# Second block's attention: heads in pairs, the rotary scores of an even and an odd head one right behind the other

## The reference, cut to what matters

```python
k = jnp.concatenate([k_nope, jnp.broadcast_to(k_rope[:, :, None, :], (b, l, MLA_HEADS, QK_ROPE_DIM))], axis=-1)
...
def one(qblk):                                  # blocks of 128 queries
    sc = jnp.einsum('bqhd,bkhd->bhqk', qblk, k, preferred_element_type=jnp.float32) * scale
    p = jax.nn.softmax(sc, axis=-1).astype(v.dtype)
    return jnp.einsum('bhqk,bkhd->bqhd', p, v)
```

## Time and profile before

| | |
|---|---|
| Time, 3 runs | 2943.76 us median, 2937.95 to 2945.43 |
| The profiled execution | 2945.6 us, of which its span 2943.5 us |
| Busy share of the span | PE 97%, PEld 84%, DVE 69%, ACT 39%, POOL 3% |
| Mean granted TensorE clock | 0.986 of full speed |
| Stage of the change | 998.11 to 1056.20 us of the span |

### The profile page before, as it was taken

How to read it: one execution, slowest core, us unless ns; L and a number is a source line. 1 busy time by engine, 2 the same in 40 slices (tenths; PEclk the granted TensorE clock), 3 DMA queues, 4 the chain that set the end, 5 groups by cost and what they waited for, 6 DMA issues and landing times.

```text
span 2943.5 us, 51456 instructions
## 1 busy us (share of the span) xinstructions
PE 2849.0 (97%) x19824; PEld 2462.9 (84%) x19824; DVE 2043.5 (69%) x3896; ACT 1139.3 (39%) x1795; POOL 86.2 (3%) x96
## 2 busy tenths in 40 slices
PE   8998999998999999999999999988999999999997
PEld 7885998885996669998999999865999999999986
DVE  4755884764874559997666666774999766666667
ACT  2423552432553432234444444431323444444443
POOL 0012000022000000000000000000000000000000
PEclk9999999999999999999999999999999999999999
DMA  5204883303883224424555555653442455555564
GB/s 197 101 18 175 326 314 129 115 32 115 314 326 145 86 90 162 152 88 175 183 181 181 183 184 185 237 191 143 148 166 76 166 184 183 185 185 185 183 227 154
DMA packets 79283, 498.30 MB, mean 169 GB/s; under 512 B 9264, under 2 KB 13744, under 8 KB 22320
## 3 DMA queue, kind: packets, MB, share of 16 engines
q1 hardware_dynamic: 70080, 477.73, 44.6%
q10 hardware_dynamic: 9072, 18.72, 1.8%
HBM read 485.92 MB, written 10.49 MB: 169 GB/s over the span
## 4 chain that ended last, share of the span: by engine, by line
PE 95%; DVE 3%; issue 1%; POOL 1%; ACT 1%; DMA 0%; DVEq 0%; SPq 0%; ACTq 0%; POOLq 0%
PE bank L841 24%; PE bank L853 24%; PE bank L887 7%; PE bank L2047 5%; PE bank L521 4%; PE bank L1860 4%; PE bank L2085 4%; PE bank L2094 4%; PE bank L671 3%; PE bank L738 2%; PE bank L1903 1%; PE bank L2027 1%; PE bank L2134 1%; PE bank L600 1%; PE bank L1848 1%; PE bank L815 1%
## 5 line engine op out<-in xcount | busy, mean ns | idle before, releaser
L853 PE MATMUL bank<-peer_pass_high,peer_pass_hidden 128*128 128x512 f32 x1472 | 495.5, 397 | 0.0
L841 PE MATMUL bank<-peer_pass_high,ring_r 128*128 128x256 f32 x1456 | 416.2, 286 | 0.0
L841 PE MATMUL bank<-peer_pass_high 128*128 128x256 f32 x1456 | 413.6, 284 | 0.0
L841 PE MATMUL bank<-hT_r,peer_pass_high 128*128 128x256 f32 x1456 | 411.1, 282 | 0.0
L951 DVE TENSOR_TENSOR ring_r<-ring,peer_pass_high 128x1024 fp32r<-128x1024 f32 x184 | 225.5, 1226 | 218.3 <-ACT peer_pass_high L1539 218.3
L853 PEld LDWEIGHTS bank<-peer_pass_high,peer_pass_hidden 128*128 128x128 f32 x1472 | 278.1, 189 | 58.8
L1539 ACT ACTIVATE peer_pass_high<-ring 128x1024 fp32r<-128x1024 f32 x184 | 195.4, 1062 | 300.7 <-DMA ring<-in_experts 299.6
L853 PE MATMUL bank<-ring_r,peer_pass_hidden 128*128 128x512 f32 x736 | 292.8, 398 | 0.0
L841 PEld LDWEIGHTS bank<-peer_pass_high 128*128 128x128 f32 x1456 | 276.8, 190 | 9.0
L841 PEld LDWEIGHTS bank<-hT_r,peer_pass_high 128*128 128x128 f32 x1456 | 277.2, 190 | 7.7
L841 PEld LDWEIGHTS bank<-peer_pass_high,ring_r 128*128 128x128 f32 x1456 | 276.7, 190 | 0.0
(11 more groups left out here) (389 smaller groups left out, 5565.1 us busy)
## 6 DMA issues: line engine op xcount, KB each, us to landing
ring<-in_experts SPq DMA_DIRECT2D x256, 1024.0 KB, 4.8
ring<-in_w SPq DMA_DIRECT2D x137, 1024.0 KB, 4.8
sb<-in_w_mod SPq DMA_DIRECT2D x48, 1024.0 KB, 6.7
sb<-spill SPq DMA_DIRECT2D x36, 256.0 KB, 5.0
spill<-sb ACTq DMA_DIRECT2D x10, 512.0 KB, 6.9
sb<-in_ln ACTq DMA_DIRECT2D x8, 512.0 KB, 4.7
spill<-sb ACTq DMA_DIRECT2D x32, 128.0 KB, 1.8
sb<-in_post ACTq DMA_DIRECT2D x4, 512.0 KB, 4.7
```

The lines of the kernel that those rows point to most:

```text
L841: m = pe.matmul(ps[u][:, 0:S], w, h[:, kt, :], start=(kt, i) == (0, 0), stop=(kt, i) == (KT - 1, 2))
L853: m = pe.matmul(ps[4 + 2 * tb + half][:, :], g[:, t], w, start=False, stop=False, skip_group_check=True)
```

## The change

The 16 units are taken in another order: `unit(n)` maps n to a head and a query block so that four successive units are head 2g, head 2g + 1 (first query block), head 2g, head 2g + 1 (second query block). Two units are scored together: the 128-row matmul of both, then the 64-row matmul of both. PE scores a pair after each odd n, where it scored one unit after each n. The products with the values come at n % 4 == 3 and n % 4 == 0, where they came at every even n; DVE takes them out at n % 4 == 0 and 1, the last two behind the loop. The job list follows. ACT's loop changes only in which head and block it takes. The number and the shapes of all instructions stay.

```diff
+def unit(n):
+
+    return 2 * (n // 4) + n % 2, n // 2 % 2
...
     for n in range(2 * MH):
         j += [(("pt", n), "act")]
-        j += [(("o", n // 2 - 1), "dve")] * (n % 2 == 0 and n > 0)
+        j += [(("o", n // 2 - 1), "dve")] * (n % 4 == 3) + [(("o", n // 2 - 1), "dve")] * (n % 4 == 0 and n > 0)
...
-    def score(n):
-        h, qb = n // 2, n % 2
-        r = (h % 2) * ROPE
-        b = SCORE_BANK + n % SCORES
-        if n >= SCORES:
-            pe.wait_ge(k.s_read, n - SCORES + 1)
-        m = pe.matmul(ps[b][:, :], k.qn[:, h, qb * P:(qb + 1) * P], k.kn[:, h, :], start=True, stop=False)
-        rel.pay(m)
-        pe.matmul(ps[b][:, :], k.qr[r:r + ROPE, h // 2, qb * P:(qb + 1) * P], k.kr[r:r + ROPE, :], start=False, stop=True)\
-          .then_inc(k.s_filled, 1)
+    def score_pair(n):
+        for i in (n, n + 1):
+            h, qb = unit(i)
+            if i >= SCORES:
+                pe.wait_ge(k.s_read, i - SCORES + 1)
+            m = pe.matmul(ps[SCORE_BANK + i % SCORES][:, :], k.qn[:, h, qb * P:(qb + 1) * P], k.kn[:, h, :], start=True, stop=False)
+            rel.pay(m)
+        for i in (n, n + 1):
+            h, qb = unit(i)
+            rows = slice((h % 2) * ROPE, (h % 2 + 1) * ROPE)
+            pe.matmul(ps[SCORE_BANK + i % SCORES][:, :], k.qr[rows, h // 2, qb * P:(qb + 1) * P], k.kr[rows, :], start=False, stop=True)\
+              .then_inc(k.s_filled, 1)
 
     def attend(h):
-        J.evac(pe, ("pt", 2 * h + 1))
+        J.evac(pe, ("pt", 4 * (h // 2) + 2 + h % 2))
...
-    for n in range(SCORES):
-        score(n)
+    for n in range(0, SCORES, 2):
+        score_pair(n)
...
-        if n + SCORES < 2 * MH:
-            score(n + SCORES)
-        if n % 2 == 0 and n:
+        if n % 2 and n + SCORES < 2 * MH:
+            score_pair(n + SCORES - 1)
+        if n % 4 == 3 or n % 4 == 0 and n:
             attend(n // 2 - 1)
...
-        if n % 2 and n > 1:
-            take_o(n // 2 - 1)
+        if n % 4 < 2 and n > 1:
+            take_o(2 * (n // 4) - 2 + n % 4)
         if n in LOW_BESIDE:
             w_low(k, v, "mla", LOW_BESIDE[n], k.mla_high, LOW_BESIDE[n] - 4)
     w_low(k, v, "mla", 10, k.mla_high, 6)
+    take_o(MH - 2)
     take_o(MH - 1)
...
     for n in range(2 * MH):
-        h, qb = n // 2, n % 2
+        h, qb = unit(n)
```

## The result

The changed kernel is slower by a third of a percent: 2950.99 us median of 8 runs (2948.02 to 2964.64) against 2941.4 us (2937.95 to 2945.43), ratio 1.0036, 95% interval [1.0025, 1.0047]. Two more series gave 1.0034 [1.0021, 1.0047] and 1.0018 [1.0006, 1.0029]. All 28 times of it, three single executions included, have a median of 2949.2 us and spread over 24 us; the kernel before spreads over 12. The forecast was +4.7 us and no change that can be told. The time fell inside the range; the size was too small, by 1.7 us in the stage (6.4 against 4.7) and by 5 in the medians of the first series (9.6 against 4.7).

What follows compares the result with a forecast made beforehand. PE was taken to bound the kernel: waits of +14.3 us against 9.5 us less work, walked as +4.7 us on 2943.76, gave 2948.5 us, range 2942.5 to 2955.

Steps and rivals of the forecast that it cites:

- What bounds the kernel: Whole program: PE is busy 97% of the span, so work or waits on PE reach the end one for one.
- PE's own work: Attention: scoring in pairs and fewer changes of rows shrink PE's work by 9.4 to 9.5 us.
- the second rotary score: Second head's 64-row score in each pair: nearly free on other row groups, taken as 0.01 us; 0.87 if fully serial.
- First and second wait: PE waits for DVE's scaling: 1.63 us at n = 0, 2, 6, 10 and 0.89 at n = 1, 3, 7, 11; together 10.0.
- Third: PE's wait at n = 5 and 9, behind DVE's taking out and weight subtraction: 2.55 us, twice, 5.1 together.
- The tail: PE's waits at the attention's end: 0.35 us at n = 13, about 0.95 at n = 14, 1.7 together with smaller ones.
- The sum: Attention stage: waits +14.3 us and work -9.5 give +4.8; walked with every start in order, +4.7.
- PE's busy time: PE's work in the attention stage was to fall from 55.3 to about 46 us.
- Rival (b): TensorE's clock falls in the attention's waits: one fall gives +7.1 to +8.1 us, two or more +9.5 to +11.5; chance 0.14.
- the bound of 0.3%: Whole kernel's time: the smallest difference a measurement can tell from no change, 8.8 us.
- The chance of 0.17 for slower: Whole kernel slower by more than 0.3%: most of (b), a third of serial rotary scores with scatter, a little else.

Runs made afterwards that it cites:

- late_both: Changed kernel with maxima n + 1 and n + 2 behind the odd unit's scaling, and both heads of a pair taken out behind those maxima: ratio 0.9965, 2932.0 us.
- filler: Changed kernel with extra matmuls in PE's waits in the attention, written into the bank the transposes then overwrite: ratio 1.0013 to the kernel before.
- low_59: Changed kernel with the two weight subtractions beside n = 5 and 9 instead of 4 and 8: ratio 1.0001 to the kernel before.
- look1: Single profiled execution of the changed kernel with no edit: attention stage 67.7 us, with three stretches at half clock.

## Why the prediction was right, and what it missed

- What bounds the kernel: right. The stages behind took 1887.1 to 1887.6 us in all six profiles of the changed kernel, 1887.3 before, so what the stage gained or lost reached the end; late_both took 10.6 us off the stage and 9.3 off the median.
- PE's own work: a pair was to take 2.89 us, it takes 2.88; the second rotary score was taken as free by the earlier trace rows, and it is (1.06 us for four MATMULs, 1.91 on one group of rows). The strict program order that the Trainium skill asks for ("TensorE: Matmul & The Clock Gate", Part 3, The mechanism) does not hold here: in that order the four could not end in less than three in a row, 1.3 us. The trace's single records of these four MATMULs say the same: two start at 1012.08 and two at 1012.62, so the first of the second head started before the second of the first head, which stands ahead of it.
- First and second wait: 1.63 and 0.89 were worked out, 1.63 and 0.89 stand there from unit 2 on (1006.76 to 1008.39; 1008.88 to 1009.77); before units 0 and 1 it is 1.8 and 0.7, the same sum. Third: 2.55, and 2.55 (1017.15 to 1019.70). The tail: 0.35 and 0.95 were worked out, 0.35 and 0.9 stand there.
- The sum was +4.7; the stage without falls is +4.9 (filler). The forecast of 62.8 us for it met 63.0. PE's busy time in it was put at about 46; the one profile without a fall or filler in which most of the waits stand (low_59) has 47.1. A row that a wait follows counts longer as busy: four transposes count 0.66 us where the next matmul starts 0.49 behind their start.
- What failed is the weight given to Rival (b). It was taken as a chance of 0.14 beside the forecast; it came on top of it in six of six profiles. Its size per fall was too large (2.4 to 3.4 us for a stretch as in the earlier trace rows; here the stretch was 3.4 us long and cost 1.5), so one fall gave +6.4 and three +9.6. The argument against it was that the clock had stayed full at 3.80 of 7.00 us busy, and the prediction says that no stretch of before is made up of waits and transposes alone. That reading is wrong: this very stretch is (L1826 and, in the changed kernel, L1831 are transposes). The first row is of the kernel before, the second of the changed one, whose program is the same up to there:

```profile
917.45 1.94 PE L1826 MATMUL bank<-sb 128*128 128x128 f32 x16 [2.59 <-DVE sb L2173]
```
```profile
912.70 3.40 PE L1831 MATMUL bank<-sb 128*128 128x128 f32 x16 [2.62 <-DVE sb L2180]
```

In the kernel before, the clock stayed full there. In five of the six profiles of the changed kernel it was at half for 3.4 us at this place, and the same sixteen transposes took 3.4 to 3.6 us. So the row on which the argument stood was one execution that met no fall; in other executions the same instructions do.
- By the bound of 0.3% the first two series are slower (1.0036, 1.0034, both intervals reaching under it) and the third is not (1.0018). The chance of 0.17 for slower was too low. That the time lay only 2.5 us above the forecast of 2948.5 is in part luck: the forecast was built on 2943.76 us for the kernel before, 2.4 above the median of its eight runs, and holds no fall. The profiles account for +6.4 us, and +9.6 in one of six; the pooled medians differ by 7.9 (2949.2 less 2941.2), the first series by 9.6. Of the rest, one part would be executions with several falls, like look1. That isn't shown: the timed runs have no trace, and between the fastest and the slowest profile the stages ahead differ by 12.6 us.

## What to carry to other kernels

When units of a pipeline written out by hand are grouped, look at the consumer's stream, not only at the producer's. DVE took each maximum two units ahead of the scaling. That did no harm while scores came one by one; with pairs it put the maximum of the pair just scored ahead of a scaling whose inputs were long ready, and taking the maxima later, behind that scaling, removed the wait. Putting two steps elsewhere in the stream of the engine that had time to spare turned +4.9 us into -10.6, with PE's stream unchanged. And add up what a wait does to the clock as well: a few microseconds in which PE has only transposes and waits were followed by half clock in six profiles of six, and the stage was 1.5 us shorter with useless matmuls in the waits than with the waits left empty. A place that kept full clock in one profile is no proof that it keeps it in the next.

## What the runs showed of the hardware

- Two float32 matmuls (two MATMULs each) with 64 rows and 512 columns on different row groups, one behind the other in the stream, ran entirely side by side: 1.06 us for both, against 1.06 for one and 1.91 for two on the same rows.
- Filling PE's waits kept the granted clock at 1.00 in two profiles of two, where the same stream with empty waits fell to 0.50 for 3.4 us at least once in six of six. Both profiles with filler still have the fall among the transposes near 912, where the waits were left empty. Not every wait of 1.6 and 0.9 us does it (four pairs of them stand in each run, and mostly one fall), and low_59, which has the same ones but shorter waits before n = 5 and 9, had none in its one profile.
- Six executions of the changed kernel differ by up to 12.6 us in the first 1000 us, along with the time spent at half clock there (34 to 58 us). A single profile's span is no measure for a change of 5 us; the length of the changed stage is, to 0.2 us between the five profiles with one fall in it.
